# A streaming step of gated linear attention and latent attention: rotary queries computed turned and set in place by transfers within SBUF, the causal mask filled by VectorE, and another order of the key steps

## The reference

```python
# layer A: gated linear attention (4 heads), residual; layer B reads one shared latent K/V side
ckv   = rmsnorm(h @ kv_w_down[:, :256]);  krope = rope(h @ kv_w_down[:, 256:], pos)
k     = concat(ckv @ w_uk (8 heads x 128), krope (64, the same for all heads));  v = ckv @ w_uv
q     = rmsnorm(h @ w_in[:, :384]) @ w_uq          # 8 heads x (128 + 64)
q     = concat(q[..., :128], rope(q[..., 128:], pos))
rope(x) = concat(x1*cos - x2*sin, x2*cos + x1*sin)  # x1, x2: halves of 32
s     = (q . k) / sqrt(192);  s = where(key_chunk <= query_chunk, s, -inf)   # chunks of 64
y     = x + rmsnorm((softmax(s) @ v * silu(gate)) @ w_out)
```

## Time and profile before

| | |
|---|---|
| median of three executions | 620.95 us |
| the profiled execution, its own time | 620.64 us |
| its span | 618.9 us |
| PE (tensor engine) busy | 599.2 us, 97% |
| PEld (its weight loads) busy | 576.6 us, 93% |
| DVE (VectorE) busy | 369.4 us, 60% |
| ACT (ScalarE) busy | 308.1 us, 50% |
| POOL (GpSimd) busy | 109.8 us, 18% |
| granted clock of the tensor engine | 0.999 |

### The profile page before, as it was taken

One profiled execution on the slowest core, in us unless ns is written; L12 is line 12 of the kernel. 1 busy time (PEld: TensorE's weight loads), 2 busy tenths in 40 slices (PEclk: granted clock), 3 DMA queues, 4 the chain that ended last, 5 costly groups with the idle time before them and its releaser, 6 DMA issues.

```text
span 618.9 us, 11804 instructions
## 1 busy us (share of the span) xinstructions
PE 599.2 (97%) x4546; PEld 576.6 (93%) x4546; DVE 369.4 (60%) x574; ACT 308.1 (50%) x616; POOL 109.8 (18%) x173
## 2 busy tenths in 40 slices
PE   8999999999999999999999999999999988799996
PEld 7999999999999999999999999989998977699996
DVE  5485667464554872277536478467788875663415
ACT  6796463442362562267326324345656567662311
POOL 0100010010030143156407200110000033400002
PEclk9999999999999999999999999999999999999999
DMA  8932362271262273242425222231110155856004
GB/s 299 348 97 87 101 204 78 73 216 54 78 203 70 79 271 104 61 147 87 135 51 156 69 69 61 60 90 31 35 53 18 51 172 203 252 176 238 1 2 170
DMA packets 65431, 73.46 MB, mean 119 GB/s; under 512 B 8160, under 2 KB 57568, under 8 KB 65248
## 3 DMA queue, kind: packets, MB, share of 16 engines
q1 hardware_dynamic: 65376, 72.71, 36.8%
HBM read 61.92 MB, written 10.78 MB: 117 GB/s over the span
## 4 chain that ended last, share of the span: by engine, by line
PE 70%; DVE 12%; ACT 10%; issue 3%; DMA 3%; POOL 2%; SPq 1%; DVEq 0%; ACTq 0%; POOLq 0%
PE bank L1598 22%; PE bank L1600 21%; PE bank L1599 21%; DVE pT_lo L1297 2%; DMA x_nat<-in_x_sample_dram 2%; ACT prob L1239 2%; DVE sT_lo L1297 1%; ACT slab_hi L1033 1%; DVE slab_lo L1297 1%; PE bank L1874 1%; ACT sT_hi L1033 1%; PE bank L1645 1%; DVE rows L1293 1%; DMA x_raw<-in_xT_dram 1%; ACT qS L1033 1%
## 5 line engine op out<-in xcount | busy, mean ns | idle before, releaser
L1598 PE MATMUL bank<-slab_hi,hat_hi 128*128 128x256 f32 (+2 forms) x560 | 160.4, 286 | 1.8 <-DVE hat_lo L1297 1.0
L1600 PE MATMUL bank<-slab_hi,hat_lo 128*128 128x256 f32 (+2 forms) x560 | 159.3, 285 | 0.0
L1599 PE MATMUL bank<-slab_lo,hat_hi 128*128 128x256 f32 (+2 forms) x560 | 159.3, 285 | 0.0
L1598 PEld LDWEIGHTS bank<-slab_hi,hat_hi 128*128 128x128 f32 x560 | 105.3, 188 | 3.3 <-DVE slab_lo L1297 1.4
L1600 PEld LDWEIGHTS bank<-slab_hi,hat_lo 128*128 128x128 f32 x560 | 105.6, 189 | 0.6
L1599 PEld LDWEIGHTS bank<-slab_lo,hat_hi 128*128 128x128 f32 x560 | 105.2, 188 | 0.6
L1297 DVE TENSOR_TENSOR slab_lo<-stage,slab_hi 128x1024 fp32r<-128x1024 f32 (+3 forms) x70 | 83.7, 1196 | 26.7 <-ACT slab_hi L1033 25.5
L1598 PE MATMUL bank<-hat_hi,slab_hi 128*128 128x320 f32 x256 | 79.4, 310 | 0.7 <-DVE krL L1297 0.4
L1599 PE MATMUL bank<-hat_lo,slab_hi 128*128 128x320 f32 x256 | 78.7, 308 | 0.0
L1600 PE MATMUL bank<-hat_hi,slab_lo 128*128 128x320 f32 x256 | 78.7, 308 | 0.0
L1033 ACT ACTIVATE slab_hi<-stage 128x1024 fp32r<-128x1024 f32 (+3 forms) x70 | 71.0, 1014 | 6.1 <-DMA stage<-in_a_w_in_dram 1.5
(11 more groups left out here) (324 smaller groups left out, 1369.7 us busy)
## 6 DMA issues: line engine op xcount, KB each, us to landing
stage<-in_a_w_in_dram SPq DMA_DIRECT2D x22, 512.0 KB, 4.6
st_s<-in_state_gla_dram SPq DMA_DIRECT2D x4, 1024.0 KB, 6.7
out_dram<-st_s SPq DMA_DIRECT2D x4, 1024.0 KB, 5.1
stage<-in_a_w_out_dram SPq DMA_DIRECT2D x8, 512.0 KB, 4.3
stage<-in_b_w_in_dram SPq DMA_DIRECT2D x8, 512.0 KB, 4.5
stage<-in_ckvT_dram SPq DMA_DIRECT2D x8, 512.0 KB, 4.0
stage<-in_cache_ckv_dram SPq DMA_DIRECT2D x8, 512.0 KB, 6.5
stage<-in_b_w_out_dram SPq DMA_DIRECT2D x8, 512.0 KB, 4.2
```

Source lines behind the costliest of these rows:

```text
L1598: pe.matmul(out, a[0], b[0], start=first, stop=False)
L1599: pe.matmul(out, a[0], b[1], start=False, stop=False)
L1600: return pe.matmul(out, a[1], b[0], start=False, stop=last)
```

## The change

The rotary queries of the prompt are computed with the head dimension as rows: `qr` of group g (four heads) and half e (x1 or x2 of the rotation) is one bank of 9 products 512 wide, from weights put in that order on the host (`uq_rope`, now two contiguous transfers). VectorE turns a group by six operations 512 wide with tables `cosT`, `sinT` (two transfers of 256 KB, step `ldt`), step `qh` splits the result into hi (ScalarE) and lo (VectorE), and 16 transfers per group of 32 partitions by 512 (64 KB each), issued by the sync engine, set it into `qS`. The samples' tile keeps the old way (`qo`, `qoT`). `qh` of the second group waits on ScalarE for the first group's 16 transfers; `qabs` of head 0 and each `S` wait for all 32. Bank numbers shift with the steps.

The mask matmuls go; in each unit's `S` VectorE first writes the large negative number into the two blocks of PSUM (64 partitions, 2 x 64 columns) and waits for it before the maxima.

In the order: at t = 5 `xT` of tile 2 stands ahead of `rs` of tile 4; `ct` of streams 0 and 1 comes a head later; `cr` and `ot` of streams 0 and 1 stand ahead of `O` of head 5; in a sample step `cr` and `ot` of stream b+3 come ahead of its `ct`, the weight piece comes last, and `Oh` of head 7 stands in step 0 behind `ct`. The staging buffers, and with them the places at which the sync engine issues the keys' loads, follow from that order; `cr` and `ct` of stream 5 are now loaded as soon as those of stream 2 are converted.

```diff
@@ -190,10 +190,10 @@
+        if NT <= t < NT + 3:
+            out += [("xT", "B", t - 3)]
...
-        if NT <= t < NT + 3:
-            out += [("xT", "B", t - 3)]
@@ -212,15 +212,15 @@
-    out += [("gb", 2, 0), ("cT", 4)] + [("qT", t) for t in range(NT)] + [("gb", 2, 1)]
-    out += [("qr", 0)]
+    out += [("gb", 2, 0), ("cT", 4)] + [("qT", t) for t in range(NT)] + [("ldt",), ("gb", 2, 1)]
+    out += [("qr", 0, 0)]
...
-    out += [("qr", 1), ("qr", 2), ("qrT", 0), ("gb", 1, 0), ("qrT", 1), ("qr", 3), ("qrT", 2), ("qr", 4)]
+    out += [("qr", 0, 1), ("gb", 1, 0), ("qh", 0), ("qr", 1, 0)]
...
-    out += [("gb", 1, 1), ("qrT", 3)]
+    out += [("qr", 1, 1), ("qo",), ("gb", 1, 1), ("qoT",)]
...
-    out += [("gb", 0, 0), ("qrT", 4), ("gb", 0, 1)]
+    out += [("qh", 1), ("gb", 0, 0), ("gb", 0, 1)]
@@ -242,34 +242,30 @@
+        if h == 5:
+            out += [("zr", 0), ("cr", 0), ("ot", 0), ("cr", 1), ("ot", 1)]
...
-            out += [("O", h)] + [("Oh", h)] * (h != 6)
+            out += [("O", h)] + [("Oh", h)] * (h < 6)
...
-        if h in (3, 4):
-            out += [("ct", h - 3)]
-        elif h == 5:
-            out += [("zr", 0), ("cr", 0), ("ot", 0), ("cr", 1), ("ot", 1)]
+        if h in (4, 5):
+            out += [("ct", h - 4)]
...
-        if b in (2, 4):
-            out += [("piece", ("wo", "B", 0), b // 2 - 1)]
-        elif b in (5, 6):
-            out += [("piece", "uv", b - 5)]
-        elif b == 7:
-            load(("wo", "B", 1))
...
-            out += [("ct", b + 3), ("cr", b + 3), ("ot", b + 3)]
+            out += [("cr", b + 3), ("ot", b + 3), ("ct", b + 3)]
+        if b == 0:
+            out += [("Oh", HB - 1)]
@@ -277,6 +273,12 @@
+        if b in (2, 4):
+            out += [("piece", ("wo", "B", 0), b // 2 - 1)]
+        elif b in (5, 6):
+            out += [("piece", "uv", b - 5)]
+        elif b == 7:
+            load(("wo", "B", 1))
@@ -883,6 +892,21 @@
+                elif kind == "ldt":
+                    after(sp, "pe", "qT", NT - 1)
+                    for to, x in ((cosT, "cosT"), (sinT, "sinT")):
+                        sp.dma_start(to[:, :], dram[x]).then_inc(tables_in, 16)
+                elif kind == "qh":
+                    g = step[1]
+                    after(sp, "dve", "qh", g)
+                    if g == 0:
+                        sp.wait_ge(kept_out, 16 * NT)
+                    for i, x in enumerate((rot_hi, rot_lo)):
+                        for e in range(2):
+                            to = qS[i * ROPE + e * RH:i * ROPE + (e + 1) * RH, :, :]
+                            for h in range(4):
+                                sp.dma_start(raw(to[:, 4 * g + h, :]), raw(x[e][h * RH:(h + 1) * RH, :])).then_inc(rotary_in, 16)
@@ -1218,12 +1242,16 @@
-                elif kind == "qrT":
-                    t = step[1]
-                    if t == 0:
-
-                        act.wait_ge(kept_out, 16 * NT)
-                    last = copy(rotary_to(t, slice(0, ROPE)), rotary_from(row, t))
+                elif kind == "qh":
+                    g = step[1]
+                    after(act, "dve", "qr", g, 1)
+                    if g:
+                        act.wait_ge(rotary_in, 16 * 16 * g)
+                    for e in range(2):
+                        last = copy(rot_hi[e][:, :], rot[e][:, :])
+                elif kind == "qoT":
+                    act.wait_ge(kept_out, 16 * NT)
+                    last = copy(rotary_to(slice(0, ROPE)), rotary_from(row))
@@ -1232,6 +1260,9 @@
                 elif kind == "qabs":
+                    if step[1] == 0:
+                        act.wait_ge(rotary_in, 16 * 32)
@@ -1524,19 +1555,37 @@
                 elif kind == "qr":
-                    t = step[1]
-                    if t > 1:
-                        after(dve, "pe", "qrT", t - 2)
-                    elif t == 0:
+                    g = step[1]
+                    if g == 0:
...
+                        dve.wait_ge(tables_in, 32)
...
-                    v = bank[:, 0, :].rearrange("p (h n) -> p h n", n=ROPE)
-                    tables = [times(cst(n)[:, t * RH:(t + 1) * RH], HB) for n in ("cos", "sin")]
-                    last = rotate(qrn[t % 2][:, :].rearrange("p (h n) -> p h n", n=ROPE), v, tables, rtmp)
-                elif kind == "qrT":
-                    t = step[1]
-                    last = low(rotary_to(t, slice(ROPE, P)), rotary_from(row, t), rotary_to(t, slice(0, ROPE)))
+                        after(dve, "pe", "krq", NT - 1)
+                    x, y = (banks(("qr", g, e))[0][:, 0, :] for e in range(2))
+                    cos, sin, t1, t2 = (v[:, :] for v in (cosT, sinT, *turn))
+                    tt(t1, x, cos, MUL)
+                    link(tt(t2, y, sin, MUL))
+                    link(tt(rot[0][:, :], t1, t2, SUB))
+                    tt(t1, y, cos, MUL)
+                    link(tt(t2, x, sin, MUL))
+                    last = tt(rot[1][:, :], t1, t2, ADD)
+                elif kind == "qh":
+                    for e in range(2):
+                        last = low(rot_lo[e][:, :], rot[e][:, :], rot_hi[e][:, :])
+                elif kind == "qo":
+                    x, y = (bank[:, 0, :].rearrange("p (g e h r) -> p g e h r", g=2, e=2, r=RH)[:, :, e, :, :] for e in range(2))
+                    to = [qrn[:, :].rearrange("p (g h n) -> p g h n", g=2, n=ROPE)[:, :, :, e * RH:(e + 1) * RH] for e in range(2)]
+                    t1, t2 = (turn[0][:, i * 256:(i + 1) * 256].rearrange("p (g h r) -> p g h r", g=2, r=RH) for i in range(2))
+                    cos, sin = (cst(n)[:, NP * RH:NT * RH].unsqueeze(1).unsqueeze(1).to_broadcast([P, 2, 4, RH]) for n in ("cos", "sin"))
...
+                elif kind == "qoT":
+                    last = low(rotary_to(slice(ROPE, P)), rotary_from(row), rotary_to(slice(0, ROPE)))
@@ -1546,6 +1595,8 @@
                 elif kind == "qabs":
+                    if step[1] == 0:
+                        dve.wait_ge(rotary_in, 16 * 32)
@@ -1553,6 +1604,10 @@
                 elif kind == "S":
...
+                    i0, i1 = UNITS[u]
+                    apart = 512 + (i1 - i0) * P
+                    link(dve.memset(row[0:P // 2, i0 * P:i0 * P + 2 * apart].rearrange("p (j n) -> p j n", n=apart)[:, :, P // 2:P], NEG))
@@ -1778,18 +1833,21 @@
                 elif kind == "qr":
-                    t = step[1]
+                    _, g, e = step
...
+                    w = [x[:, g * PIECE:g * PIECE + KQ * 256].rearrange("p (k n) -> p k n", n=256)[:, :, e * P:(e + 1) * P] for x in weights("uqr")]
+                    for k in range(KQ):
+                        last = mm3(bank[:, 0, :], cut(w, A_, k), cut(qlT, A_, k, slice(0, SEQ)), k == 0, k == KQ - 1)
+                elif kind == "qo":
...
-                            last = mm3(bank[:, 0, g * 256:(g + 1) * 256], cut(qlT, A_, k, slice(t * P, (t + 1) * P)), cut(w, A_, k), k == 0, k == KQ - 1)
-                elif kind == "qrT":
-                    t = step[1]
-                    after(pe, "dve", "qr", t)
+                            last = mm3(bank[:, 0, g * 256:(g + 1) * 256], cut(qlT, A_, k, slice(SEQ, TOK)), cut(w, A_, k), k == 0, k == KQ - 1)
+                elif kind == "qoT":
+                    after(pe, "dve", "qo")
...
-                        last = pe.transpose(row[0:ROPE, h * P:(h + 1) * P], qrn[t % 2][:, h * ROPE:(h + 1) * ROPE], ident)
+                        last = pe.transpose(row[0:ROPE, h * P:(h + 1) * P], qrn[:, h * ROPE:(h + 1) * ROPE], ident)
@@ -1819,16 +1877,15 @@
-                    after(pe, "dve", "qrT", NT - 1)
+                    pe.wait_ge(rotary_in, 16 * 32)
+                    after(pe, "dve", "qoT")
...
-                        pe.matmul(o, qS[:, h, q], krL[:, keys], start=False, stop=False)
-
-                        last = pe.matmul(bank[:, j, q], cst_r("early"), cst_r("late"), start=False, stop=True)
+                        last = pe.matmul(o, qS[:, h, q], krL[:, keys], start=False, stop=True)
```

More of the change, by code:

```diff
@@ L51 @@
 CONST, NCONST = columns((("ident", P), ("mask_p", P), ("mask_s", P), ("parity", 2), ("cos", NT * RH), ("sin", NT * RH)))
-CONST_R, NCONST_R = columns((("cum_p", P + 2), ("cum_s", P + 2), ("early", P), ("late", P)))
+CONST_R, NCONST_R = columns((("cum_p", P + 2), ("cum_s", P + 2)))
 def slabs():
@@ L77, in slabs @@
     gb = {("gb", s): halves("b_w_in", QL + s * 256, "b_norm_pre") for s in range(4)}
-    uqr = [[("uq_rope", 0, KQ, h * ROPE, 4 * ROPE, "b_q_norm")] for h in (0, 4)]
+    uqr = [[("uq_rope", 0, KQ, g * 4 * ROPE, 4 * ROPE, "b_q_norm")] for g in range(2)]
     for name in (("gb", 3), ("gb", 2), "uqr", ("gb", 1), ("gb", 0)):
@@ L311, in parts @@
         return ("pe", "act")
+    if step[0] == "qr" and step[2] == 0:
+        return ("pe",)
     if step in APART:
@@ L382, in stage_counts @@
         for w, k0, k1, *_ in windows:
-            count[STAGE_OF[n]] += 16 * (k1 - k0 if w == "uq_rope" else 1)
+            count[STAGE_OF[n]] += 16
```

(26 more changed lines are left out.)

29 lines of the change are left out of this document (14 added, 15 removed).

## The result

The changed kernel takes 628.07 us in the median of seven runs (625.66 to 630.36), the kernel before, run beside it, 622.10 us (620.44 to 624.13). The ratio is 1.0092, with a 95% interval of 1.0071 to 1.0113: 0.9%, some 5.7 us, slower. The forecast was 619.6 us. The profiled execution of the changed kernel is one of 628.07 us (span 626.2), 7.4 us over that of before.

A forecast was written before the change was run, and what follows sets the result against it. Bounds taken: PE in the rotary stretch, VectorE in the prompt heads, an ACT-VectorE ring in the samples. From 620.64 us, -1.0 - 3.5 + 1.3 + 1.9 = -1.3 gave 619.3, 619.6 on the median's footing; range 616.2 to 622.8.

The forecast's parts named there:

- part 2's line for VectorE: Rotary stretch: VectorE ends the turning 0.5 us before PE's samples' transposes, so no wait; 1 us later would cost 0.5.
- Rival D: Slower: VectorE late at samples' transposes, memset and samples at upper ends, no xT gain; 623.6 us, chance 0.07.
- Part 1: xT ahead of rs at tile 5: PE's wait for hat_lo shrinks, gain 1.0 us, bounds 0 and 1.24.
- Part 2, PE's side: Rotary queries: fewer transposes -3.6, wider products -0.2, longer wait at gb(1,0) +0.3; -3.5 us in all.
- Rival C: Slower: the 32 transfers run one after another on the sync queue and S(0,0) waits; 625.5 us, chance 0.07.
- Part 3: Prompt heads: mask fill on VectorE, fewer PE matmuls and the later ct together cost +1.3 us, ends -0.1 and +2.7.
- the memset: VectorE's mask fill, two per head, 0.32 us each with hand-over, lower end 0.21; heads bound by VectorE grow 0.4.
- ct's new place: Heads: moving ct of streams 0 and 1 a head later takes off 1.26 us and adds 0.3.
- Part 4: Samples: the new step order lengthens the steps, +1.87 us in sum, bounds +1.0 and +2.5; the end moves by it.
- skS in the ring: Sample steps: with cr ahead of ct, skS stands between spT and sT_hi in the closed ACT-VectorE cycle, +0.66 us.
- A: Heads: memset short or hidden in VectorE's waits, heads come to -0.1; 618.2 us; this, B or both 0.36.
- B: Samples: their ACT-VectorE cycle does not grow because skS finds a gap; 617.7 us; A, this or both 0.36.

The follow-up runs named there:

- E1: The changed kernel with the weight pieces of gb 0 placed behind qr(1,1) and qo in the order; 620.65 us, ratio to before 0.9994.
- H1: The changed kernel with 16 extra 512-wide products keeping PE busy ahead of the samples' transposes' wait for qo; 624.55 us, ratio to before 1.0062.
- E4: The kernel before with only xT moved ahead of rs at tile 5; 620.38 us, ratio to before 0.9986.
- E3: The changed kernel with the mask added by PE matmuls again, no VectorE memset, new ct order kept; 624.94 us, ratio to before 1.0055.
- F1: The changed kernel with gb 0's pieces behind qo and the samples' order of before; 618.28 us, ratio to before 0.9952.
- F4: E1 with ct put back ahead of cr in the samples, the rest of their new order kept; 617.75 us, ratio to before 0.9951.
- E2: The changed kernel with the whole samples' order of before, heads keeping their new order; 623.59 us, ratio to before 1.0038.
- G1: The kernel before with xT moved and the new rotary part, gb 0's pieces behind qo; 617.47 us, ratio to before 0.9939.
- H2: F4 with the mask on PE matmuls again; 616.31 us, ratio to before 0.9925.

## Why the prediction was wrong

**The step that failed** is part 2's line for VectorE: "From 372.7 (behind slab_lo of gb 0) these end at 379.4, and PE's transposes of the samples come at 379.9: 0.5 us to spare, no wait". VectorE ended slab_lo of gb 0 at 379.2 in an execution that came to the rotary stretch 2.2 us later than that of before, so at 377.0 on the prediction's own clock: 4.3 us later than its 372.7, of which 4.13 are the idle time in front. Its ACT half can't start before PE has read the last of uq_rope, which is in the same slab. I had dated the weight piece by the engine that does it and left out who still reads what it overwrites. Before the change this was free: the pieces stood behind the last reader's step, and nobody waited for VectorE behind them. Then the price: "should VectorE be 1 us later, it costs 0.5" was right about the wait (4.3 late less 0.5 to spare is 3.8, and PE waited 3.74; it would have come at 380.0 on the prediction's clock, forecast 379.9) and had nothing for the clock. E1 takes both away (6.1 us by ratio, 4.97 in the trace); H1 takes the clock's part alone (1.9 by ratio, 1.3 in the trace). Rival D had this place and no such size: 623.6 against 628.

**Part 1**: forecast -1.0. E4 has -0.9 by ratio, 0.26 in its trace; of the right sign, perhaps too large.

**Part 2, PE's side**: forecast -3.5. E1's trace has -3.36, and the wait at gb(1,0) 0.92 against 0.65. Right, once the stall is cured. The 32 transfers were hidden, as forecast, though slower to issue:

```profile
372.58 5.04 SPq L909 DMA_DIRECT2D qS<-rot_hi  x8
377.66 5.03 SPq L909 DMA_DIRECT2D qS<-rot_lo  x8
...
394.83 4.96 SPq L909 DMA_DIRECT2D qS<-rot_hi  x8
399.83 5.02 SPq L909 DMA_DIRECT2D qS<-rot_lo  x8
```

That is 0.63 us per issue, not 0.52; the last issue ends at 404.85, a transfer lands 2.0 us behind its issue in the median (3.0 at most), and S(0,0) starts at 417.96 without a wait. Rival C, which began at 1.0 us each, did not happen. The fixed cost that the prediction took from the Trainium skill (DMA: Bandwidth & Descriptors, section Anatomy of one DMA) stands there for transfers issued by GpSimd; these, issued by the sync engine, took the same 2.0 us each, but one was issued every 0.63 us, so it was a latency and did not add up.

**Part 3**: forecast +1.3 for the heads; +0.26 in head 0's approach, +0.60 in the heads and 0.31 of the samples' row, which is the memset's too by E3: +1.17 in all. That it came so near is in part luck. E3, which has the new place of ct(0) and ct(1) but no memset, splits the heads: the mask costs +1.17 there where I had +2.26, and ct's new place brings -0.57 (81.78 against 82.35) where I had -0.96. The term that was mis-sized is the memset: 0.20 us with its hand-over where I took 0.32, below even the lower end of 0.21; and in the second interval, where I had VectorE lead already, the change gained 0.27, as if PE still led. The lesson is in the choice of the row: I took a 64x128 operation that reads two operands, one of them from PSUM, and a fill reads none. That this is the reason was not tested.

**Part 4**: forecast +1.87 up to the exponentials that free PE's bank, the seventh sample's, and "the end moves by this sum". From head 7's first exponential to the seventh sample's it is 40.10 us before, 42.75 changed and 42.45 in E3: +2.35 without the memset's share, and at the end E3 has +2.40 over before. So the end did move by the sum, and the sum was 0.5 too small. The mechanism, skS in the ring with 0.66, was exact to 0.01, but in E3 step 0 came to +0.85, step 1 to +0.75, steps 2 and 3 together to +1.28 and step 4 to -0.51, where I had +0.73, +0.66, +1.11 and -0.63; why each is 0.1 to 0.2 more stays open. By ratio it is 2.6 (F1 against E1). The table's +2.17 up to the last exponential and +0.53 behind it cut this at another place. F4 against F1 shows that the +0.53 goes with the new place of the weight pieces and Oh(7): it has 70.06 us behind the last first-exponential against 69.57, but the last exponential comes 0.85 sooner behind the heads (45.14 against 45.99), so this place costs nothing in sum (F4's trace is 0.36 us shorter here).

**The rivals**: A had the memset right (short), not its sum for the heads; B is out, skS found no gap; C did not happen; D named the place. Without the stall the forecast would have been near: the cured kernel takes 620.65 us against 619.6.

## What to carry to other kernels

When work in an engine's order is dated, ask for each piece what its destination still holds and who reads that last; a conversion that writes over a slab ends no sooner than the slab's last reader, and everything behind it in the same engine's order waits with it. Put what PE needs next ahead of such a piece: here two lines of order were worth 6.1 us, more than all that the change was to bring. And price a stall of PE of some microseconds at more than its length: here a wait of 3.74 us cost 3.65 with the clock kept and 1.3 to 1.6 more in the two profiled executions in which the clock fell behind it.

## What the runs showed of the hardware that was not expected

- The granted clock fell behind a wait of 3.74 us, but not each time: two profiled executions show 0.83 for that 10 us window, one shows 1.00 behind the same wait (E2). The run medians, 0.9935 to 0.995 with the wait and 0.9975 to 0.9985 without it or with PE kept busy through it, show it better than any one trace: 21 of the 25 runs with the wait are at 0.996 or less, and 10 of 71 runs of the kernel before. In the changed kernel's trace the clock was at the lower of its two levels, 1.2 GHz, for a good two microseconds behind the wait.
- The same 60 us of products ran at 87 or 88 starts per 10 us in three of 14 profiled executions and at 90 or 91 in the others, at a granted clock shown as 1.00. G1's and H2's profiled executions, two of the three, took 619.06 and 618.44 us where their medians are 617.47 and 616.31. What makes the difference was not found. It is worth 1.7 us, as much as most effects studied here, so two single traces can't be subtracted without a look at a stretch that both share.
- Transfers within SBUF of 64 KB over 32 partitions: 0.63 us each to issue on the sync engine's queue, 2.0 us from issue to landing in the median, so that several were under way at once.
- A VectorE fill of 64 partitions x 128 fp32 elements in PSUM took 0.165 us, with 0.03 us to the next operation; an elementwise operation of the same shape with one operand in PSUM took 0.278 in the kernel before.
